# Rotation of the retention q and k: on GpSimd, or on VectorE in two steps

## The chip, the cores and the metric

The kernel runs on one core of one Trainium2 chip. The metric is device time in microseconds (us) of one execution; lower is better. TensorE (PE) multiplies, VectorE (DVE), ScalarE (ACT) and GpSimd (POOL) do the elementwise work, and SyncE (SP), ACT and POOL issue the transfers (DMA).

## The reference, cut to what matters

Two layers of a hybrid decoder block on 256 tokens of width 1024, all in float32. Each layer has a SwiGLU half step, one combined projection into three branches (retention, sliding-window attention, attention into 256 memory tokens), a gated sum of the branches, an output projection and a second SwiGLU half step. The change concerns one step of the retention branch, the rotation of its q and k (4 heads of 128 each) by position:

```
def rotary(x):
    ...
    x1, x2 = x[..., :half], x[..., half:]
    return jnp.concatenate([x1 * cos - x2 * sin, x1 * sin + x2 * cos], axis=-1)
...
    q = rotary(q.astype(f32))
    k = rotary(k.astype(f32)) * (dk ** -0.5)
...
    s = jnp.einsum('bnchd,bnshd->bnhcs', qc, kc) * intra_decay
```

## The kernel before, in words

**Weights.** All large products run in three passes of TensorE (lines 761 to 763): each float32 weight is split into a high and a low part. A weight block of 128x2048 (1 MB) is loaded by SP into a slot of `raw` (three slots, here also `raw_x`), ACT makes `w_hi` from it (line 1169, two pieces of 128x1024), and DVE makes `w_lo` as the difference (line 1563, two pieces). Each of those pieces on DVE counts up the semaphore `weights_made`, on which SP's next loads wait. `w_hi` and `w_lo` have three slots too, so ACT and DVE make the weights of an item up to three items before TensorE uses them.

**Quarter sums.** Pairs of projections (`rk` is the pair of retention q and k) are computed with seven products in place of eight, numbered 1 to 7. For some of them the weight is a sum of two blocks, made by DVE (line 1560) or by a transfer of POOL that adds into the slot (line 668).

**Order.** The order inside the mixing part is one list of names, `SCHEDULE`, that every engine walks through, each doing its own part of each name. An engine does its instructions strictly in that order. A name like `rk:4` is a product, `rv0.1` the second half of a projection, and a plain name is a step. After an item's own work ACT and DVE make the weights that the item's freed slot takes. Around the change the list reads, before:

```
... pv0 rk:7 e1 rv0.0 s2 rk:4 rg:5 rot pt1 rg:1 rqt pv1 rv0.1 e2 s3 rv1.0 e3 rg:3 pt2 rg:6 ...
```

Of these, `rot` is the rotation; `rqt` transposes the rotated q on TensorE (line 818) and waits for it (semaphore `rotated`); `rkt`, some items later, does the same for k. `s2` and `s3` are scores of the sliding window (line 969), `e1` to `e3` their exponentials on ACT, `pt1` the transposes of the probabilities (line 981), and `pv0`, `pv1` the products with the values (lines 993 and 995), which DVE scales into `stA` (lines 1816, 1818, 1825). The small products rotate through four PSUM banks, so that `s2` takes a bank that `pv0` leaves, and `s3` one that `pv1` leaves: TensorE can't start `s3` before DVE has done line 1825 of `pv1`.

**The rotation.** It is done in place in `stB`, per 128 tokens and for q and k (four tiles of 128x512 a layer): `rot_a` is the tile times the cosines (line 699), `rot_b` the swapped halves times the sines (line 702, two instructions of 4 heads x 64), and their sum goes back to `stB` (line 706). The scratch `rot_a` and `rot_b` lies over memory from which the memory values were written out by the transfer `mv_kept<-mv_made`, so the first tile waits for that (`mv_stored`).

Of the kernel before, what the change touches and what calls it, by code (L numbers as in the profile page):

```python
# [30 lines left out]
P = 128  # L31
# [42 lines left out]
MIX_PAIRS = {"sq": ("sq0", "sq1"), "rk": ("rq0", "rk0"), "rv": ("rv0", "rv1"), "rg": ("rg0", "rg1"),  # L74
             "gs": ("gs0", "gs1"), "mq": ("mq0", "mq1"), "gr": ("gr0", "gr1"), "gm": ("gm0", "gm1")}
SCHEDULE = """
mk0.1+xt0 mk1.0+xt1 mk1.1 skv.0 sq0.0 S_sum sq1.0 S_hi S_lo mkt sq1.1 sq0.1 skt mv0.0 sqt rk:5 mv0.1 s0 mv1.0 s1 e0 rk:1 rk:3 pt0 rk:6 mv1.1 mv_out rk:2 pv0 rk:7 e1 rv0.0 s2 rk:4 rg:5 rot pt1 rg:1 rqt pv1 rv0.1 e2 s3 rv1.0 e3 rg:3 pt2 rg:6 rv1.1 rkt rg:7 pv2 rg:2 rg:4 pt3 gs:5 rs gs:1 pv3 gs:3 gs:6 st gs:2 gs:7 us0.0 gs:4 ro us0.1 us1.0 mq1.0 us1.1 re mq1.1 mq0.0 mq0.1 gr:5 mqt gr:3 gr:1 rt mkT_in gr:6 gm0.0 gr:7 gr:2 gr:4 mv_in ms me ur0.0 mn x_in ur0.1 gm0.1 ur1.0 mpt gm1.0 ur1.1 mpv um0.0 um0.1 gm1.1 um1.0 mg0 um1.1 wo0.0 mg1 wo1.0 wo0.1 wo1.1+yt0
""".split()

PAIR_OF, STEPS = {}, []  # L80
# [278 lines left out]
def build(nc, x_in, mem_in, memt_in, stream, gains_in, gfin_in, rot_in, decay_in, mask_in, ident_in, out):  # L359
# [6 lines left out]
    with ctx:  # L366
# [279 lines left out]
        @block.gpsimd  # L646
        def _(pool):
            pool.memset(still[:, :], 0.0).then_inc(still_ready, 1)
            pool.memset(eps[:, :], EPS).then_inc(pool_step, 1)
            pool.memset(mhalf[:, :], -0.5).then_inc(pool_step, 1)  # L650
            pool.memset(minus[:, :], -1.0).then_inc(pool_step, 1)
            pool.wait_ge(pool_step, 3)

            def inv_rms(dst, src, n, done, step):

                pool.tensor_tensor(dst[:, 0:n], src[:, 0:n], eps[:, 0:n], ALU.add).then_inc(pool_step, 1)
                pool.wait_ge(pool_step, step)
# [12 lines left out]

            def quarters_after(l, i):
                if ITEMS[l][i] == ("down", 2, DOWNS[l, 2][-1]):
                    quarters_after(l, i - 1)
                for o in split_after[l * NI + i]:
                    add_quarters(o)

            PER = 5 + 4 * 3
            for l in range(DEPTH):
                def at(n):
                    return l * PER + (3 + n)  # L680

                def ffn(f):
                    for s in ffn_steps(l, f):
                        if s[0] != "gt" and s != ("down", f, DOWNS[l, f][-2]):
                            quarters_after(l, AT[l][s])

                n = 3

                def rotate(qk, t):
                    nonlocal n  # L690
                    pool.wait_ge(*done_of(l, ("rq0", "rk0")[qk], t))
                    src = stB[:, t, qk * BLK:(qk + 1) * BLK].rearrange("p (h d) -> p h d", h=RET_H)
                    av = rot_a[:, :].rearrange("p (h d) -> p h d", h=RET_H)
                    bv = rot_b[:, :].rearrange("p (h d) -> p h d", h=RET_H)
                    half = RET_DK // 2
                    cos = rot[:, 0, t].unsqueeze(1).broadcast_to([P, RET_H, P])
                    if n > 3:
                        pool.wait_ge(rotated, l * 4 + (qk * TT + t))
                    pool.tensor_tensor(av, src, cos, ALU.mult).then_inc(pool_step, 1)
                    for lo, hi in ((0, half), (half, 0)):  # L700
                        sin = rot[:, 1, t, lo:lo + half].unsqueeze(1).broadcast_to([P, RET_H, half])
                        pool.tensor_tensor(bv[:, :, lo:lo + half], src[:, :, hi:hi + half], sin, ALU.mult)\
                            .then_inc(pool_step, 1)
                    n += 3
                    pool.wait_ge(pool_step, at(n))
                    pool.tensor_tensor(src, av, bv, ALU.add).then_inc(rotated, 1)

                pool.wait_ge(msq_ready, l * 3 * TT + TT)
                inv_rms(rstd, msq, TT, rstd_ready, at(1))
                if l == 0:  # L710
                    for dst, src in ((rot, rot_in), (decay, decay_in), (mask, mask_in)):
                        pool.dma_start(dst[:], src).then_inc(tables_loaded, 16)
                ffn(1)
                pool.wait_ge(mem_msq_ready, l * TT + TT)
                inv_rms(rstd_mem, msq_mem, TT, rstd_mem_ready, at(2))
                pool.wait_ge(msq_ready, l * 3 * TT + 2 * TT)
                inv_rms(rstd, msq, TT, rstd_ready, at(3))
                pool.wait_ge(rstd_ready, l * 3 + 2)
                pool.tensor_tensor(minus_rstd[:, :], rstd[:, :], minus[:, :], ALU.mult).then_inc(minus_ready, 1)
                pool.wait_ge(tables_loaded, 16 * 3)  # L720
                for s in STEPS:
                    if s[0] != "step":
                        quarters_after(l, AT[l][s if s[0] == "prod" else ("mix", s[1])])
                    elif s[1] == "rot":
                        pool.wait_ge(mv_stored, 16 * (l + 1))
                        for qk in range(2):
                            for t in range(TT):
                                rotate(qk, t)
                    elif s[1] == "ro":
                        pool.wait_ge(retsq_ready, l * 2 * RET_H + 2 * RET_H)  # L730
                        inv_rms(rstd_r, msq_r, 2 * RET_H, retstd_ready, at(n + 1))
                pool.wait_ge(msq_ready, l * 3 * TT + 3 * TT)
                inv_rms(rstd, msq, TT, rstd_ready, at(n + 2))
                assert n + 2 == PER
                ffn(2)

            for t in range(TT):
                r = rstd[:, t:t + 1]
                pool.wait_ge(end_mean, t + 1)
                pool.tensor_tensor(r, r, mhalf[:, 0:1], ALU.pow).then_inc(end_rstd, 1)  # L740
# [795 lines left out]
        def _(dve):  # L1536
# [177 lines left out]
            for l in range(DEPTH):  # L1714
# [39 lines left out]
                def product(k, n):  # L1754

                    if n not in (2, 6, 7):
                        return
                    t, j = QUARTERS[n]
                    name, other = f"p0_{k}_{n}", {2: 1, 6: 3, 7: 5}[n]
                    buf = {"sq": stB, "rk": stB, "rv": rv, "rg": srg, "mq": stA}.get(k, gates)  # L1760
                    dst = buf[:, t, j * BLK:(j + 1) * BLK]
                    taken = snap_late[other][:, :] if k in ("gr", "gm") else dst
                    dve.wait_ge(minus_ready, l + 1)
                    dve.wait_ge(*full(l, name))
                    dve.wait_ge(*out_of(l, f"p0_{k}_{other}"))
                    if n == 2:
                        i = nc.vector.scalar_tensor_tensor(dst, bank(name)[:, :], rstd[:, t:t + 1], taken, op0=ALU.mult, op1=ALU.add)
                    else:
                        i = nc.vector.scalar_tensor_tensor(dst, bank(name)[:, :], minus_rstd[:, t:t + 1], taken, op0=ALU.mult, op1=ALU.subtract)
                    i.then_inc(free(name), 1)  # L1770

                def step(s):
                    if s == "S_sum":
                        left_sums(l, 0, hM)
                    elif s == "S_lo":
                        left_parts(l, 0)
# [205 lines left out]
```

## Time and profile before

| | |
|---|---|
| time, median of 3 runs | 1474.6 us (1473.6 to 1475.37) |
| time of the profiled execution | 1475.33 us |
| its span, from first to last instruction | 1473.5 us |
| busy: TensorE / VectorE / ScalarE / GpSimd | 98% / 77% / 65% / 8% of the span |
| mean granted TensorE clock | 0.992 of full speed |

The span is what the trace shows of the execution; 1.8 us of its time lie around it. TensorE works nearly without a gap, so what matters are the few places at which it waits, what it waits for there, and the stretches behind them in which its clock is lower. The layers are alike: the rotation comes at about 295 us in the first and at about 1020 us in the second.

### The profile page before, as it was taken

Reading aid. Unit: us, or ns where it says so; the run is one execution under the profiler, and the core shown is the slowest. Engines: PE = TensorE matmul, PEld = TensorE weight load, DVE = VectorE, ACT = ScalarE, POOL = GpSimd, SP = SyncE. Lnnn points to the kernel's source line nnn. Section 1 sums busy time; section 2 is a strip of 40 time slices with the busy share of each in tenths; the row PEclk is TensorE's granted clock in tenths of the full one; section 3 lists DMA queues with packets and bytes.
Section 4 is the critical chain, followed back from the end, with each engine's and each line's share of the span. In section 5 each row is a group of like instructions: output and inputs, shape, how many; then the busy total and the mean of one; then the engine's idle time right before and its main releaser. Section 6 shows DMA issues by size and latency. Waiting matters only on the chain.

```text
span 1473.5 us, 17927 instructions
## 1 busy us (share of the span) xinstructions
PE 1442.0 (98%) x6838; PEld 1195.7 (81%) x6838; DVE 1134.8 (77%) x1266; ACT 960.0 (65%) x1412; POOL 116.7 (8%) x125
## 2 busy tenths in 40 slices
PE   8999999989999999999999999999899999999997
PEld 6888888868888888888888888888688888888886
DVE  6998755797677658798789986568786885688994
ACT  6777666667647447676677775668675664476673
POOL 0000000070000000000000000002500000010000
PEclk9999999999999999999999999999999999999999
DMA  9999648855847557889939987567666564778881
GB/s 368 261 280 275 249 158 287 230 150 170 257 130 274 196 184 273 260 250 308 324 118 286 296 222 278 203 207 222 168 193 236 177 235 159 294 205 270 276 267 43
DMA packets 49380, 340.37 MB, mean 231 GB/s; under 512 B 5552, under 2 KB 6192, under 8 KB 8848
## 3 DMA queue, kind: packets, MB, share of 16 engines
q1 hardware_dynamic: 37392, 259.54, 46.8%
q0 software_dynamic: 8624, 61.74, 21.6%
q10 hardware_dynamic: 3280, 17.95, 3.2%
q8 instruction: 55, 0.90, 0.2%
q14 instruction: 29, 0.24, 0.0%
HBM read 331.87 MB, written 7.34 MB: 230 GB/s over the span
## 4 chain that ended last, share of the span: by engine, by line
PE 86%; DVE 7%; DMA 3%; ACT 2%; issue 1%; SPq 1%; POOLq 0%; POOL 0%; DVEq 0%; ACTq 0%
PE bank L761 26%; PE bank L763 26%; PE bank L762 26%; DVE w_lo L1563 4%; PE bank L818 4%; DMA raw<-in_stream 2%; DMA raw_q<-in_stream 1%; ACT w_hi L1169 1%; PE bank L1096 1%; PE bank L1078 1%; DVE raw_x L1560 1%; PE bank L969 1%; ACT prob L1469 1%; PE bank L995 0%; SPq L622 0%
## 5 line engine op out<-in xcount | busy, mean ns | idle before, releaser
L1563 DVE TENSOR_TENSOR w_lo<-raw,w_hi 128x1024 fp32r<-128x1024 f32 x356 | 428.0, 1245 | 179.4 <-ACT w_hi L1169 178.8
L1169 ACT ACTIVATE w_hi<-raw 128x1024 fp32r<-128x1024 f32 x356 | 356.8, 1053 | 210.7 <-PE bank L763 192.1
L761 PE MATMUL bank<-w_hi,hT_lo 128*128 128x512 f32 (+1 forms) x716 | 280.7, 392 | 0.5 <-DVE hT_lo L1587 0.2
L763 PE MATMUL bank<-w_lo,hT_hi 128*128 128x512 f32 (+1 forms) x716 | 276.3, 386 | 0.0
L762 PE MATMUL bank<-w_hi,hT_hi 128*128 128x512 f32 (+1 forms) x716 | 276.2, 386 | 0.0
L761 PEld LDWEIGHTS bank<-w_hi,hT_lo 128*128 128x128 f32 x716 | 135.1, 189 | 30.9 <-issue 3.7
L763 PEld LDWEIGHTS bank<-w_lo,hT_hi 128*128 128x128 f32 x716 | 134.9, 188 | 27.4
L762 PEld LDWEIGHTS bank<-w_hi,hT_hi 128*128 128x128 f32 x716 | 135.2, 189 | 25.4
L761 PE MATMUL bank<-w_hi,S_lo 128*128 128x512 f32 x340 | 135.4, 398 | 1.1 <-ACT snap L1250 0.8
L763 PE MATMUL bank<-w_lo,S_hi 128*128 128x512 f32 x340 | 132.8, 390 | 0.0
L762 PE MATMUL bank<-w_hi,S_hi 128*128 128x512 f32 x340 | 132.4, 389 | 0.0
L761 PE MATMUL bank<-w_hi,bT_lo 128*128 128x512 f32 x320 | 126.8, 396 | 0.0
L763 PE MATMUL bank<-w_lo,bT_hi 128*128 128x512 f32 x320 | 124.7, 390 | 0.0
L762 PE MATMUL bank<-w_hi,bT_hi 128*128 128x512 f32 x320 | 124.6, 389 | 0.0
L761 PE MATMUL bank<-w_hi,gT_lo 128*128 128x512 f32 x256 | 101.3, 396 | 4.6 <-DVE gT_lo L1581 4.5
L763 PE MATMUL bank<-w_lo,gT_hi 128*128 128x512 f32 x256 | 100.5, 392 | 0.0
L762 PE MATMUL bank<-w_hi,gT_hi 128*128 128x512 f32 x256 | 100.2, 391 | 0.0
L1563 DVE TENSOR_TENSOR w_lo<-raw_q,w_hi 128x1024 fp32r<-128x1024 f32 x70 | 82.5, 1220 | 13.0 <-ACT w_hi L1169 13.0
L1563 DVE TENSOR_TENSOR w_lo<-raw_b,w_hi 128x1024 fp32r<-128x1024 f32 x68 | 80.1, 1219 | 9.6 <-ACT w_hi L1169 9.6
L1169 ACT ACTIVATE w_hi<-raw_b 128x1024 fp32r<-128x1024 f32 x68 | 68.3, 1054 | 24.9 <-PE bank L763 11.8
L1169 ACT ACTIVATE w_hi<-raw_q 128x1024 fp32r<-128x1024 f32 x70 | 70.3, 1055 | 21.6 <-PE bank L763 16.6
L761 PEld LDWEIGHTS bank<-w_hi,S_lo 128*128 128x128 f32 x340 | 63.9, 188 | 14.3 <-ACT snap L1250 1.5
(229 smaller groups left out, 2461.4 us busy)
## 6 DMA issues: line engine op xcount, KB each, us to landing
raw<-in_stream SPq DMA_DIRECT2D x158, 1024.0 KB, 5.8
raw_b<-in_stream SPq DMA_DIRECT2D x33, 1024.0 KB, 8.0
raw_q<-in_stream SPq DMA_DIRECT2D x33, 1024.0 KB, 9.0
raw<-in_stream POOLq DMA_DIRECT2D x30, 1024.0 KB, 9.1
raw_x<-in_stream SPq DMA_DIRECT2D x20, 1024.0 KB, 5.1
raw_b<-in_stream POOLq DMA_DIRECT2D x15, 1024.0 KB, 10.2
raw_q<-in_stream POOLq DMA_DIRECT2D x11, 1024.0 KB, 12.0
raw<-in_stream SPq DMA_DIRECT2D x8, 256.0 KB, 6.9
```

The source lines that it names most:

```text
L761: nc.tensor.matmul(dst, xl, wh[:, a:b], start=first, stop=False, skip_group_check=more)
L762: nc.tensor.matmul(dst, xh, wh[:, a:b], start=False, stop=False, skip_group_check=more)
L763: return nc.tensor.matmul(dst, xh, wl[:, a:b], start=False, stop=last, skip_group_check=more)
L818: last = nc.tensor.transpose(bank(name)[:, at:at + P], src(t, k0 + j), ident[:, :])
L969: last = nc.tensor.matmul(bank(name)[:, i * n:(i + 1) * n], sqT[rows, head // 2, tokens(b)], skT[rows, head // (SWA_H // SWA_KV), 0:n], st ...
L1078: last = nc.tensor.matmul(bank(name)[:, t * MEM:(t + 1) * MEM], mqT[:, 2 * h + k, tokens(t)], mkT[:, 2 * h + k, :], start=k == 0, stop=k == 1)
L1096: last = nc.tensor.matmul(bank(name)[:, j * SEQ:(j + 1) * SEQ], mv[:, m, k * P:(k + 1) * P], mpT[:, h, m, :], start=m == 0, stop=m == 1)
L1169: nc.scalar.activation(slots(o)[0][:, part], raw_slot(s)[:, part], ACT.Copy).then_inc(hi_split, 1)
L1469: last = nc.scalar.activation(p, p, ACT.Exp, bias=snm[:, g % 2, i, b:b + 1], accum_out=ssum[:, g % 2, i, b:b + 1])
L1560: nc.vector.tensor_tensor(raw_slot(to[0]), raw_slot(to[0]), raw_slot(plus[0]), ALU.add).then_inc(weights_made, 1)
L1563: nc.vector.tensor_tensor(lo[:, part], raw_slot(s)[:, part], hi[:, part].bitcast(F32), ALU.subtract)\
```

## The change

The step `rot` of GpSimd becomes two steps, `rotq` and `rotk`, of VectorE, at the same place of the list. VectorE does the same four instructions a tile, with the same waits; within a tile the last one waits for the second multiplication by the sines through `dve_step`, and each tile's first waits for the sum of the tile before (`rotated`). Two waits are added in front of VectorE's products of the gates `gr` and `gm`; they wait for VectorE's own earlier work.

```diff
-... e1 rv0.0 s2 rk:4 rg:5 rot pt1 rg:1 rqt pv1 ...
+... e1 rv0.0 s2 rk:4 rg:5 rotq rotk pt1 rg:1 rqt pv1 ...
...
-                    elif s[1] == "rot":
-                        pool.wait_ge(mv_stored, 16 * (l + 1))
-                        for qk in range(2):
-                            for t in range(TT):
-                                rotate(qk, t)
...
+                    if k == "gr":
+                        dve.wait_ge(*out_of(l, f"us{j}t{t}"))
+                    if k == "gm":
+                        dve.wait_ge(gates_used, l * 8 + (TT * j + t + 1))
...
+                def rotate(qk, t):
+
+                    dve.wait_ge(*done_of(l, ("rq0", "rk0")[qk], t))
+                    src = stB[:, t, qk * BLK:(qk + 1) * BLK].rearrange("p (h d) -> p h d", h=RET_H)
+                    av = rot_a[:, :].rearrange("p (h d) -> p h d", h=RET_H)
+                    bv = rot_b[:, :].rearrange("p (h d) -> p h d", h=RET_H)
+                    half = RET_DK // 2
+                    if qk or t:
+                        dve.wait_ge(rotated, l * 4 + (qk * TT + t))
+                    nc.vector.tensor_tensor(av, src, rot[:, 0, t].unsqueeze(1).broadcast_to([P, RET_H, P]), ALU.mult)
+                    for lo, hi in ((0, half), (half, 0)):
+                        sin = rot[:, 1, t, lo:lo + half].unsqueeze(1).broadcast_to([P, RET_H, half])
+                        i = nc.vector.tensor_tensor(bv[:, :, lo:lo + half], src[:, :, hi:hi + half], sin, ALU.mult)
+                    own(i)
+                    settled()
+                    nc.vector.tensor_tensor(src, av, bv, ALU.add).then_inc(rotated, 1)
+
                 def step(s):
-                    if s == "S_sum":
+                    if s in ("rotq", "rotk"):
+                        dve.wait_ge(mv_stored, 16 * (l + 1))
+                        for t in range(TT):
+                            rotate(int(s == "rotk"), t)
+                    elif s == "S_sum":
```

On VectorE, from the weights made behind `rk:4` and `rg:5` to the scaling of `pv1`, the kernel before has these rows (the brackets name the semaphores waited for):

```order
L1563 TENSOR_TENSOR w_lo<-raw,w_hi 128x1024 [waits hi_split] x4
L1560 TENSOR_TENSOR raw_x<-raw_x,raw 128x2048 [waits weights_made,raw_loaded2,raw_loaded7]
L1563 TENSOR_TENSOR w_lo<-raw,w_hi 128x1024 [waits hi_split] x2
L1816 TENSOR_TENSOR ssum<-ssum,sexp 128x8 [waits swa_exp]
L1818 RECIPROCAL ssum<-ssum 128x8 [waits dve_step]
L1825 TENSOR_TENSOR stA<-bank,ssum 128x256 [waits psum_full4,dve_step]
```

The changed kernel has at the same place (first tile of q, first of k, and what follows; line numbers are 27 or 2 lower here for the same code):

```order
L1536 TENSOR_TENSOR w_lo<-raw,w_hi 128x1024 [waits hi_split] x4
L1758 TENSOR_TENSOR rot_a<-stB,rot 128x512 [waits psum_free3,mv_stored]
L1761 TENSOR_TENSOR rot_b<-stB,rot 128x4x64 x2
L1764 TENSOR_TENSOR stB<-rot_a,rot_b 128x512 [waits dve_step]
...
L1758 TENSOR_TENSOR rot_a<-stB,rot 128x512 [waits rotated,psum_free2,mv_stored]
...
L1533 TENSOR_TENSOR raw_x<-raw_x,raw 128x2048 [waits weights_made,raw_loaded2,raw_loaded7]
L1536 TENSOR_TENSOR w_lo<-raw,w_hi 128x1024 [waits hi_split] x2
L1814 TENSOR_TENSOR ssum<-ssum,sexp 128x8 [waits swa_exp]
L1816 RECIPROCAL ssum<-ssum 128x8 [waits dve_step]
L1823 TENSOR_TENSOR stA<-bank,ssum 128x256 [waits psum_full4,dve_step]
```

Sixteen instructions a layer now stand in VectorE's queue between the four `w_lo` pieces and everything behind them; the order of the rest is as it was. On GpSimd, from the reciprocal of the norm on, the kernel before has

```order
L719 TENSOR_TENSOR minus_rstd<-rstd,minus 128x2
L668 DMA raw<-in_stream 128x2048 x3
L699 TENSOR_TENSOR rot_a<-stB,rot 128x512
L702 TENSOR_TENSOR rot_b<-stB,rot 128x4x64 x2
L706 TENSOR_TENSOR stB<-rot_a,rot_b 128x512
```

and the changed kernel

```order
L698 TENSOR_TENSOR minus_rstd<-rstd,minus 128x2
L668 DMA raw<-in_stream 128x2048 x4
L668 DMA raw_x<-in_stream 128x2048
L668 DMA raw<-in_stream 128x2048 x2
L656 TENSOR_TENSOR rstd_r<-msq_r,eps 128x8
```

so that GpSimd's fourth adding transfer no longer stands behind the rotation. TensorE's, ScalarE's and SyncE's rows are the same in both.

## Rows read from the trace of the kernel before

**Rows 1.** The page's busy time of each engine.

```profile
PE 1442.0 (98%) x6838; PEld 1195.7 (81%) x6838; DVE 1134.8 (77%) x1266; ACT 960.0 (65%) x1412; POOL 116.7 (8%) x125
```

**Rows 2.** Waits of TensorE: us in total, times, longest.

```profile
PE bank L969 <- DVE stA L1825: 13.8, 3, 6.7
```

**Rows 3.** Timeline, TensorE, both layers: start, us, instructions, [idle before <-releaser].

```profile
298.93 1.58 PE L969 MATMUL bank<-skT,sqT 64*128 64x128 f32 x16 [0.69 <-DVE stA L1825]
310.11 1.04 PE L818 MATMUL bank<-ident,stB 128*128 128x128 f32 x8
...
325.62 2.93 PE L969 MATMUL bank<-skT,sqT 64*128 64x128 f32 x16 [6.34 <-DVE stA L1825]
...
1035.02 1.03 PE L818 MATMUL bank<-ident,stB 128*128 128x128 f32 x8
...
1050.95 2.93 PE L969 MATMUL bank<-skT,sqT 64*128 64x128 f32 x16 [6.73 <-DVE stA L1825]
```

**Rows 4.** Timeline, VectorE around the rotation, first layer, then one row of the second.

```profile
291.45 2.29 DVE L1560 TENSOR_TENSOR raw_x<-raw_x,raw 128x2048 f32<-128x2048 f32 x1 [2.08 <-DMA raw<-in_stream]
...
301.93 2.35 DVE L1563 TENSOR_TENSOR w_lo<-raw,w_hi 128x1024 fp32r<-128x1024 f32 x2
...
308.56 7.91 DVE L1563 TENSOR_TENSOR w_lo<-raw,w_hi 128x1024 fp32r<-128x1024 f32 x4
316.39 3.37 DVE L1560 TENSOR_TENSOR raw_x<-raw_x,raw 128x2048 f32<-128x2048 f32 x1
319.69 3.41 DVE L1563 TENSOR_TENSOR w_lo<-raw,w_hi 128x1024 fp32r<-128x1024 f32 x2
...
324.72 0.76 DVE L1825 TENSOR_TENSOR stA<-bank,ssum 128x256 f32<-128x256 f32 x2 [0.23 <-DVE ssum L1818]
...
1035.21 6.78 DVE L1563 TENSOR_TENSOR w_lo<-raw,w_hi 128x1024 fp32r<-128x1024 f32 x4
```

**Rows 5.** Timeline, GpSimd: the rotation's first instruction, and the one behind its last.

```profile
294.77 1.29 POOL L699 TENSOR_TENSOR rot_a<-stB,rot 128x512 f32<-128x512 f32 x1 [22.07 <-DMA mv_kept<-mv_made]
...
324.17 0.89 POOL L668 DMA_DIRECT2D raw<-in_stream  x1
```

**Rows 6.** Single lines of VectorE: duration min/median/max in ns, first and last start.

```profile
L1563 DVE TENSOR_TENSOR w_lo<-raw,w_hi x356: 1208/1219/2341, 17.6 to 1446.7; 128x1024 fp32r<-128x1024 f32 x178
L1816 DVE TENSOR_TENSOR ssum<-ssum,sexp x8: 159/431/1253, 297.1 to 1097.5; 128x8 f32<-128x8 f32 x8
L1825 DVE TENSOR_TENSOR stA<-bank,ssum x16: 414/420/425, 298.0 to 1098.3; 128x256 f32<-128x256 f32 x16
L1811 DVE TENSOR_TENSOR ssink<-gains,smax x8: 159/160/1277, 268.7 to 1057.4; 128x8 f32<-128x8 f32 x8
```

**Rows 7.** Timeline, VectorE where 128x512 operations follow each other from SBUF.

```profile
230.09 0.69 DVE L1598 TENSOR_TENSOR S_sum<-hM 128x512 f32<-128x512 f32 x1
230.81 0.69 DVE L1600 SCALAR_TENSOR_TENSOR S_sum<-S_sum,hM 128x512 f32<-128x512 f32 x1
231.42 0.69 DVE L1602 TENSOR_TENSOR S_sum<-hM 128x512 f32<-128x512 f32 x1
```

**Rows 8.** Busy time by stretch; the column before the DMA share is the granted clock.

```profile
324.00:324.50 0.50, 0.00 (x0) 0.00 (x0) 0.45 (x2) 0.50 (x4) 0.50 (x2) 0.89 0.00 0
331.00:331.50 0.50, 0.50 (x3) 0.36 (x3) 0.50 (x1) 0.00 (x0) 0.00 (x0) 0.78 1.39 197
1048.00:1048.50 0.50, 0.00 (x0) 0.00 (x0) 0.50 (x1) 0.50 (x3) 0.50 (x1) 0.52 0.00 0
1054.50:1055.00 0.50, 0.50 (x3) 0.40 (x2) 0.50 (x2) 0.00 (x0) 0.00 (x0) 0.65 0.86 180
```

**Rows 9.** Timeline, ScalarE: high parts of the weights.

```profile
299.31 1.99 ACT L1169 ACTIVATE w_hi<-raw 128x1024 fp32r<-128x1024 f32 x2
...
335.60 2.01 ACT L1169 ACTIVATE w_hi<-raw 128x1024 fp32r<-128x1024 f32 x2 [10.10 <-PE bank L763]
...
1024.78 1.99 ACT L1169 ACTIVATE w_hi<-raw 128x1024 fp32r<-128x1024 f32 x2
```

More of the change, by code:

```diff
@@ L76 @@
 SCHEDULE = """
-mk0.1+xt0 mk1.0+xt1 mk1.1 skv.0 sq0.0 S_sum sq1.0 S_hi S_lo mkt sq1.1 sq0.1 skt mv0.0 sqt rk:5 mv0.1 s0 mv1.0 s1 e0 rk:1 rk:3 pt0 rk:6 mv1.1 mv_out rk:2 pv0 rk:7 e1 rv0.0 s2 rk:4 rg:5 rot pt1 rg:1 rqt pv1 rv0.1 e2 s3 rv1.0 e3 rg:3 pt2 rg:6 rv1.1 rkt rg:7 pv2 rg:2 rg:4 pt3 gs:5 rs gs:1 pv3 gs:3 gs:6 st gs:2 gs:7 us0.0 gs:4 ro us0.1 us1.0 mq1.0 us1.1 re mq1.1 mq0.0 mq0.1 gr:5 mqt gr:3 gr:1 rt mkT_in gr:6 gm0.0 gr:7 gr:2 gr:4 mv_in ms me ur0.0 mn x_in ur0.1 gm0.1 ur1.0 mpt gm1.0 ur1.1 mpv um0.0 um0.1 gm1.1 um1.0 mg0 um1.1 wo0.0 mg1 wo1.0 wo0.1 wo1.1+yt0
+mk0.1+xt0 mk1.0+xt1 mk1.1 skv.0 sq0.0 S_sum sq1.0 S_hi S_lo mkt sq1.1 sq0.1 skt mv0.0 sqt rk:5 mv0.1 s0 mv1.0 s1 e0 rk:1 rk:3 pt0 rk:6 mv1.1 mv_out rk:2 pv0 rk:7 e1 rv0.0 s2 rk:4 rg:5 rotq rotk pt1 rg:1 rqt pv1 rv0.1 e2 s3 rv1.0 e3 rg:3 pt2 rg:6 rv1.1 rkt rg:7 pv2 rg:2 rg:4 pt3 gs:5 rs gs:1 pv3 gs:3 gs:6 st gs:2 gs:7 us0.0 gs:4 ro us0.1 us1.0 mq1.0 us1.1 re mq1.1 mq0.0 mq0.1 gr:5 mqt gr:3 gr:1 rt mkT_in gr:6 gm0.0 gr:7 gr:2 gr:4 mv_in ms me ur0.0 mn x_in ur0.1 gm0.1 ur1.0 mpt gm1.0 ur1.1 mpv um0.0 um0.1 gm1.1 um1.0 mg0 um1.1 wo0.0 mg1 wo1.0 wo0.1 wo1.1+yt0
 """.split()
@@ L269 @@
 NG = G_SINK + SWA_H
-DVE_STEPS = 24
+DVE_STEPS = 28
 X_PARTS = [slice(0, BLK // 2), slice(BLK // 2, BLK), slice(BLK, D)]
@@ L675, in quarters_after @@
                     add_quarters(o)
-            PER = 5 + 4 * 3
+            PER = 5
             for l in range(DEPTH):
@@ L685, in ffn @@
                             quarters_after(l, AT[l][s])
[L687 to L706, printed above, removed]
                 pool.wait_ge(msq_ready, l * 3 * TT + TT)
@@ L723, in _ @@
                         quarters_after(l, AT[l][s if s[0] == "prod" else ("mix", s[1])])
-                    elif s[1] == "rot":
-                        pool.wait_ge(mv_stored, 16 * (l + 1))
-                        for qk in range(2):
-                            for t in range(TT):
-                                rotate(qk, t)
                     elif s[1] == "ro":
                         pool.wait_ge(retsq_ready, l * 2 * RET_H + 2 * RET_H)
-                        inv_rms(rstd_r, msq_r, 2 * RET_H, retstd_ready, at(n + 1))
+                        inv_rms(rstd_r, msq_r, 2 * RET_H, retstd_ready, at(4))
                 pool.wait_ge(msq_ready, l * 3 * TT + 3 * TT)
-                inv_rms(rstd, msq, TT, rstd_ready, at(n + 2))
-                assert n + 2 == PER
+                inv_rms(rstd, msq, TT, rstd_ready, at(PER))
                 ffn(2)
```

## The prediction

> **What bounds the kernel now.** I begin with the page's busy times: TensorE has 98% of the span [rows 1], so a change elsewhere counts only where it moves one of TensorE's waits. The view of waits shows what they are. Three waits of the scores (`s2`, `s3`) for VectorE's scaling `stA` come to 13.8 us [rows 2]. The timeline places them: 0.69 us at 298.93 and 6.34 us at 325.62 in the first layer, 6.73 us at 1050.95 in the second [rows 3]. All three fall beside or right behind the rotation, which GpSimd begins at 294.77 and leaves shortly before 324.17 [rows 5].
>
> Next comes VectorE's timeline at that place. From 301.93 on it has no idle time worth naming, but its instructions are longer than elsewhere. Four pieces of `w_lo` take 7.91 us, the sum `raw_x` 3.37 and two more pieces 3.41 [rows 4]. A piece takes 1.219 us in the median, a pair that nothing disturbs 2.35, and the same sum 2.29 when GpSimd is idle [rows 4, 6]; back to back, a piece costs 1.14 (it overlaps the next by 0.08) and the sum 2.21. So the three groups would take 4.64, 2.29 and 2.36 us, and the rotation beside them costs VectorE 3.27 + 1.08 + 1.05 = 5.4 us. Even tiny operations between two SBUF tiles suffer: `ssum` has a median of 0.43 and a maximum of 1.25 us against 0.16, `ssink` a maximum of 1.28 against 0.16 [rows 6]. VectorE's queue up to `stA` is what TensorE waits for, and GpSimd stretches it.
>
> The clock belongs to the wait. In the first layer it falls from full to half (2.4 to 1.2 GHz) at about 324.4, 5.1 us after TensorE stopped, and returns at about 331.2; in the second it falls at 1048.0 and returns at 1054.85 [rows 8]. Work runs at half speed from 325.62 to 331.2 and from 1050.95 to 1054.85, which loses half of these, 2.8 and 1.95 us. The place costs now 0.69 + 6.34 + 2.8 = 9.8 us in the first layer and 6.73 + 1.95 = 8.7 in the second.
>
> **The change, part by part.**
>
> *Price of the rotation on VectorE.* The trace before has no multiplication by a broadcast table here, so I take the nearest rows. A 128x512 operation takes 0.69 us; one that waits for its predecessor's result starts 0.72 behind it (0.03 of latency), one that doesn't 0.61 [rows 7]. A 128x256 operation with a broadcast operand takes 0.42, and a pair 0.76, so the first of a pair costs 0.34 [rows 4, 6]. A tile is cosines 0.61, first sines 0.34, second sines 0.42 + 0.03, sum 0.69 + 0.03: 2.12 us. q has two tiles, 4.2 us; q and k 8.4 us. Bounds: with no overlap at all 2.28 a tile (0.69 + 0.42 + 0.42 + 0.69 and 0.06), which makes q 0.3 us longer; with full overlap of every instruction 1.9 (twice 0.61 and 0.34), 0.4 shorter for q. I take 2.12, since each part is a row of the same kind and size.
>
> A rule of the Trainium skill ("VectorE: DVE Perf Modes", section on the TRN2 errata) would price an SBUF operation of N elements at 58 + N cycles of 0.96 GHz, hence 0.594 and 0.327 us, and a tile at 1.84. By it q would be 0.55 us shorter and the whole change 1.1 us better than my sum. The rows here show 0.69 for such an operation, and they decide.
>
> *VectorE's start in the first layer.* Without GpSimd's rotation the stretch from 294.77 on is shorter, but the pair at 301.93 can't start before ScalarE has the first half of its `w_hi`, made from 299.31 on in 1.05 us [rows 4, 9]; that is 300.4. So VectorE reaches the four pieces 1.5 us earlier, plus 0.1 for small operations stretched in between: 307.0 instead of 308.56 [rows 4]. Four pieces take 4.56 and the rotation starts at 311.5. The transfer that it waits for was done at 294.77 [rows 5], so that wait is free. q is ready at 315.7, and `rqt` can start 0.14 later, at 315.9 (the gap between the end of `stA` at 325.48 and the start at 325.62) [rows 3, 4].
>
> *The new wait.* TensorE reached `rqt` at 310.11 without waiting [rows 3]; now it comes 0.7 earlier, since the wait at 298.93 goes (its `stA` stands behind a stretched `ssum` [rows 6] and stretched pieces, which together give back more than 0.7). With its last product ending 0.16 after the next could start, TensorE stands from 309.6 to 315.9, 6.3 us. Queued behind are `pv1`, `rv0.1` and `s3`, 9.0 us of work (from 310.11 to 325.62 - 6.34 = 319.28, where the wait before `s3` began, less the 0.16) [rows 3]. Its clock will fall as it did for an idle time of the same length; I put down 2.5 us, between the two losses seen.
>
> *The old wait.* `rotk` 4.2, `raw_x` 2.21, two pieces 2.28, then `ssum`, the reciprocal and `stA` 1.2: `stA` is done at 315.7 + 9.9 = 325.6, as before (325.48). But TensorE comes to `s3` only at 315.9 + 9.0 + 2.5 = 327.4, so the 6.34 us there are gone. The price of `rotk` is covered by TensorE's own work, with 1.7 us to spare; without that cover each us of it would be a us of wait.
>
> *The second layer.* Four pieces started at 1035.21 [rows 4]. `ssum` and `ssink` were stretched by 1.1 us each [rows 6], and one pair of pieces between them too, but the pair behind that waits for ScalarE's half at 1024.78 + 1.05 [rows 9]; that makes 1.65 + 1.1 = 2.75 us earlier, 1032.5. Add 4.56 and 4.2: q at 1041.2, `rqt` at 1041.4 instead of 1035.02 [rows 3]. TensorE stands 6.2 us; `stA` is ready at 1051.1 and `s3` comes at 1041.4 + 9.0 + 2.5 = 1052.9, again without a wait.
>
> *The rest costs nothing.* GpSimd's fourth adding transfer may leave before 324.17 [rows 5]; nobody waited for it, ScalarE waiting for TensorE at 335.60 [rows 9]. ScalarE's `w_hi` of `raw_x` and `e2` move behind the later end of `rv0.1`, into its idle time of 10.1 us before 335.60 [rows 9]; if that were not there, they would delay the next weights by some 5 us. The added waits for `gr` and `gm` are for VectorE's own finished work. SP's next load waits for pieces that come 0.5 us later relative to TensorE, well ahead of need.
>
> **The sum.** First layer: 6.3 + 2.5 = 8.8 against 9.8, that is -1.0. Second: 6.2 + 2.5 = 8.7 against 8.7, 0. The profiled execution took 1475.33 us (span 1473.5 and 1.8 around it), which gives 1474.3; the median of the runs is 0.7 lower, so I say 1473.6 against 1474.6. The long wait is moved from `s3` to `rqt`, hardly shortened.
>
> **The rivals.**
> - *The clock stays up.* In the first layer it fell 5.1 us after TensorE stopped, in the second 3.8 [rows 3, 8]; had the fall come over 6.3 us after, the new wait would end before it. For that speaks only that the delay varies. Then `s3` waits for `stA` at 325.75, and the layer costs 325.75 less the 318.5 at which TensorE could have come, 7.2 us: -2.6 in the first and -1.5 in the second. In both layers 1470.5, in one about 1472.5.
> - *The stretching isn't GpSimd's doing* (slower). If the long `w_lo` and `raw_x` came from something else, such as transfers, the rotation would simply be put into the queue: q at 316.4 + 4.2, a wait of 10.5 us and 2.8 of clock, then `stA` at 325.5 + 8.4 = 333.9, 1.5 behind TensorE. That is +5 us in the first and +6 in the second, 1486. Against it: the stretched rows lie just where GpSimd computes, and the pair at 301.93, in its pause, took the usual 2.35 [rows 4, 5]. It decides from 1.5 us more a layer before q is ready.
> - *The queue behind is late* (slower). The `s3` masks on VectorE now end near 336.1, 0.5 after it would take up the weights of 335.60 [rows 9]. If loads behind these pieces landed late, each layer would lose 1 to 2 us: 1477.
> - *It does nothing at all.* If both waits keep their sum to within the 0.2% (2.9 us) that a measurement of this kernel can tell from no change, this can't be told from my forecast.
>
> **How the numbers follow.** Wait moved, sum kept: 0.63, with its own range of 1472.0 to 1475.5 (0.3 to 0.4 us a layer of q's price, 1 of the clock, 0.5 of the run). Clock stays up in a layer or both: 0.17, half of it beyond 0.2%. Stretching not relieved, in part or all: 0.10. Queue behind late: 0.10, half of it beyond. Over 0.2% faster also if the relief reaches work that I count as bound by ScalarE, 0.1 out of the first case. That makes faster 0.19, same 0.66, slower 0.15. The range goes down to the clock's case, 1470.4, and up to the late queue's, 1477.2.
>
> **What the profile after would show.** A wait of TensorE's line 818 for VectorE's `stB` of about 6 us at 309.5 and at 1035, and none over 1 us of line 969 for `stA`; `w_lo` with a maximum below 1.3 us everywhere; tiles of 2.1 us on VectorE; half clock for 4 to 6 us behind each wait. I am wrong if `s3` still waits for over 1 us behind a slow clock, if pieces stay stretched, or if a wait that stands in no row here appears behind 330.

## The result, and the profile after

The changed kernel takes 1479.89 us (median of 5 runs, 1477.81 to 1481.96) where the kernel before takes 1475.13 (5 runs, 1473.6 to 1475.42): a ratio of 1.0035, 95% interval 1.002 to 1.0049. It is slower, by 4.8 us. I had said 1473.6, in a range up to 1477.2.

The page's busy times and TensorE's view of waits (us in total, times, longest):
```profile
PE 1447.0 (98%) x6838; PEld 1200.4 (81%) x6838; DVE 1134.1 (77%) x1298; ACT 959.4 (65%) x1412; POOL 66.6 (5%) x93
```
```profile
PE bank L791 <- DVE stB L1764: 12.1, 2, 6.1
PE bank L734 <- DVE gT_lo L1554: 3.6, 1, 3.6
```
TensorE does the same 6838 instructions as in [rows 1], but they take 5.0 us more. The 13.8 us of waits for `stA` [rows 2] are gone; two waits for the rotated q in `stB` stand in their place. The timeline of TensorE, first layer and then the second, with the first product behind each wait and the first large one:
```profile
297.43 1.58 PE L942 MATMUL bank<-skT,sqT 64*128 64x128 f32 x16
...
314.81 1.97 PE L791 MATMUL bank<-ident,stB 128*128 128x128 f32 x8 [6.05 <-DVE stB L1764]
316.57 0.53 PE L966 MATMUL bank<-sv,pT 128*128 128x64 f32 x2
...
321.56 0.77 PE L734 MATMUL bank<-w_hi,hT_lo 128*128 128x512 f32 x1
...
324.22 0.40 PE L734 MATMUL bank<-w_hi,hT_lo 128*128 128x512 f32 x1
...
328.43 1.58 PE L942 MATMUL bank<-skT,sqT 64*128 64x128 f32 x16
...
1041.21 1.97 PE L791 MATMUL bank<-ident,stB 128*128 128x128 f32 x8 [6.00 <-DVE stB L1764]
```
Line 942 is `s2` and `s3` (line 969 in [rows 3]): neither waits now. Line 791 is `rqt`; its eight transposes took 1.04 us in [rows 3] and take 1.97 here. A large product takes 0.77 us at 321.56 and 0.40 at 324.22. That is the clock. Busy time by stretch, granted clock in the column before the DMA share:
```profile
313.00:314.00 1.00, 0.00 (x0) 0.00 (x0) 1.00 (x3) 0.00 (x0) 0.00 (x0) 0.96 1.16 467
...
318.00:323.00 5.00, 5.00 (x22) 4.71 (x22) 4.97 (x6) 0.00 (x0) 0.00 (x0) 0.50 0.00 0
324.00:324.50 0.50, 0.50 (x4) 0.39 (x3) 0.50 (x2) 0.00 (x0) 0.31 (x1) 0.84 0.00 0
1037.00:1038.00 1.00, 0.00 (x0) 0.00 (x0) 1.00 (x3) 0.82 (x1) 0.00 (x0) 0.77 0.99 418
...
1051.00:1051.50 0.50, 0.50 (x3) 0.37 (x2) 0.14 (x1) 0.00 (x0) 0.43 (x1) 0.80 0.00 0
```
A mean of 0.96 over one us means that the clock fell at 313.92, and 0.84 over half a us that it rose at 324.16; in the second layer it fell at 1037.54 and rose at 1051.2. Work ran at 1.2 GHz from 314.81 to 324.16 and from 1041.21 to 1051.2, 9.35 and 10.0 us, of which half is lost: 4.7 and 5.0. In the kernel before it was 2.8 and 1.95 [rows 8].

VectorE's timeline shows the relief and the new step:
```profile
305.94 4.63 DVE L1536 TENSOR_TENSOR w_lo<-raw,w_hi 128x1024 fp32r<-128x1024 f32 x4
310.48 0.69 DVE L1758 TENSOR_TENSOR rot_a<-stB,rot 128x512 f32<-128x512 f32 x1
311.09 0.76 DVE L1761 TENSOR_TENSOR rot_b<-stB,rot 128x256 f32<-128x256 f32 x2
311.88 0.69 DVE L1764 TENSOR_TENSOR stB<-rot_a,rot_b 128x512 f32<-128x512 f32 x1
312.67 0.69 DVE L1758 TENSOR_TENSOR rot_a<-stB,rot 128x512 f32<-128x512 f32 x1
...
314.07 0.69 DVE L1764 TENSOR_TENSOR stB<-rot_a,rot_b 128x512 f32<-128x512 f32 x1
...
319.09 2.28 DVE L1533 TENSOR_TENSOR raw_x<-raw_x,raw 128x2048 f32<-128x2048 f32 x1
321.29 2.35 DVE L1536 TENSOR_TENSOR w_lo<-raw,w_hi 128x1024 fp32r<-128x1024 f32 x2
...
323.99 0.76 DVE L1823 TENSOR_TENSOR stA<-bank,ssum 128x256 f32<-128x256 f32 x2
```
The three groups of [rows 4] went from 7.91, 3.37 and 3.41 us to 4.63, 2.28 and 2.35. `stA` is done at 324.75, before TensorE comes to `s3` at 328.43. VectorE did its part; the time went into TensorE's clock.

The place, from the waits and the half clock, costs 6.05 + 4.7 = 10.75 and 6.00 + 5.0 = 11.0, in all 21.75 us; before it was 9.8 + 8.7 = 18.5. That is +3.25. One wait elsewhere, for `gT_lo`, has 3.6 us here and had 4.5 before; in a second profile of the changed kernel (`e5_after_again`) it has 4.6, so it varies by itself. +3.25 - 0.9 gives +2.35; the two profiled executions differ by 2.5 (1477.81 against 1475.33). The second profile took 1478.93 us, +3.6: there the two waits are 6.15 and 6.14 and the work at half clock 9.3 and 10.1 us, so the place costs 22.0, +3.5. The medians differ by 4.8 and, in the 8 runs of `e5_after_again`, by 4.3; about 1 us of that has no row in either profile and stays open.

### The profile page after: what moved, and what is told of

Same layout as the page of the kernel before. It is cut to its first block, busy times and chain, and to the rows that moved or that the text cites. A ratio compares the mean times of both kernels' runs of the same rounds, so it can differ in the third digit from the quotient of the medians.

```text
span 1476.0 us, 17933 instructions
## 1 busy us (share of the span) xinstructions
PE 1447.0 (98%) x6838; PEld 1200.4 (81%) x6838; DVE 1134.1 (77%) x1298; ACT 959.4 (65%) x1412; POOL 66.6 (5%) x93
## 4 chain that ended last, share of the span: by engine, by line
PE 90%; DVE 4%; ACT 3%; DMA 2%; issue 1%; SPq 1%; POOLq 0%; POOL 0%; DVEq 0%; ACTq 0%
PE bank L734 27%; PE bank L736 27%; PE bank L735 27%; PE bank L791 4%; DVE w_lo L1536 1%; ACT w_hi L1142 1%; DMA raw_q<-in_stream 1%; PE bank L968 1%; PE bank L1051 1%; PE bank L1069 1%; DMA raw<-in_stream 1%; ACT prob L1442 1%; PE bank L966 0%; PE bank L942 0%; PE bank L954 0%
## 5 line engine op out<-in xcount | busy, mean ns | idle before, releaser
L1536 DVE TENSOR_TENSOR w_lo<-raw,w_hi 128x1024 fp32r<-128x1024 f32 x356 | 419.3, 1220 | 171.2 <-ACT w_hi L1142 170.4
L1142 ACT ACTIVATE w_hi<-raw_b 128x1024 fp32r<-128x1024 f32 x68 | 68.3, 1055 | 24.8 <-PE bank L736 11.8
L1142 ACT ACTIVATE w_hi<-raw_q 128x1024 fp32r<-128x1024 f32 x70 | 70.2, 1055 | 19.9 <-PE bank L736 15.8
L1536 DVE TENSOR_TENSOR w_lo<-raw_x,w_hi 128x1024 fp32r<-128x1024 f32 x48 | 56.6, 1220 | 32.0 <-ACT w_hi L1142 31.7
```

Source lines behind the costliest of these rows:

```text
L1142: nc.scalar.activation(slots(o)[0][:, part], raw_slot(s)[:, part], ACT.Copy).then_inc(hi_split, 1)
L1536: nc.vector.tensor_tensor(lo[:, part], raw_slot(s)[:, part], hi[:, part].bitcast(F32), ALU.subtract)\
```

## The experiments

Theory: the wait was moved as forecast, and the loss is that the clock stays low for longer behind it, because `rqt` and `pv1` follow, small products (8 transposes of 128 columns, then 24 records of 64 columns), where `s3` (16 records of 128) and then large products followed before. Counts here are those of the trace, in which each small float32 product of `pv1`, `s3` and e10 stands as two records. Rivals: the rotation on VectorE costs in other ways (its length, a queue behind), or the longer stretch belongs to the length of the wait. All ratios are against the kernel before on the same chip, whose median there was 1475.46 (e1 to e4), 1475.0 (e5 to e8), 1475.16 (e9 to e11) and 1475.61 us (e12).

| run | median us (runs) | ratio | interval |
|---|---|---|---|
| e1_after_warm | 1472.11 (7) | 0.9981 | 0.9968 to 0.9994 |
| e2_before_warm | 1471.17 (6) | 0.9966 | 0.9953 to 0.9979 |
| e3_no_rotation | 1468.72 (5) | 0.9943 | 0.9923 to 0.9963 |
| e4_dense_first | 1483.32 (4) | 1.0053 | 1.0039 to 1.0067 |
| e5_after_again | 1479.31 (8) | 1.0023 | 1.0011 to 1.0034 |
| e6_q_same_k_late | 1467.07 (5) | 0.9943 | 0.9931 to 0.9956 |
| e7_stA_first | 1472.46 (11) | 0.9982 | 0.9973 to 0.9991 |
| e8_all_behind_s3 | 1466.16 (5) | 0.994 | 0.9927 to 0.9952 |
| e9_order_alone | 1475.52 (11) | 0.9997 | 0.9988 to 1.0006 |
| e10_small_behind_wait | 1503.26 (2) | 1.019 | 1.0172 to 1.0207 |
| e11_all_hidden | 1464.46 (6) | 0.9927 | 0.9914 to 0.9939 |
| e12_rqt_later | 1461.06 (4) | 0.9903 | 0.9887 to 0.992 |

### What is the clock worth: e1 and e2

24 products without use fill the wait, ahead of `rqt` in the changed kernel:
```diff
+                        if s == "rqt":
+                            pe.wait_ge(*room(l, "rqt_0"))
+                            for _ in range(24):
+                                nc.tensor.matmul(bank("rqt_0")[:, :], still[:, 0:P], still[:, :], start=True, stop=True)
```


> The changed kernel, with 24 idle matmuls of 128x512 (bf16 zeros, into a bank that the transposes then overwrite) that TensorE runs just before it waits for the rotated q. Nothing else changes and the output is the same. Theory C (the clock): the change kept the idle time (12.1 us in two waits, against 13.8 before) but the stretch of half clock behind each wait grew to 9.3 and 10.2 us of work, a loss of 4.7 + 5.1 us against 2.8 + 1.95. With TensorE busy in the wait its clock stays at full speed, and the time falls by about 9.8 us or more, to 1468 to 1470 us, with a spread as small as before. Rival Q (something in the queues behind the rotation is late, the clock is only a by-product): the time stays at 1478 to 1480 us.

The same lines with bank `s3_1`, ahead of the wait of `s3`, in the kernel before:

> The kernel before, with the same 24 idle matmuls just before TensorE waits for the banks of s3. Theory C: this gives back the 2.8 + 1.95 us of the clock, so 1475.1 - 4.8 = about 1470.4 us; the changed kernel with warm matmuls is then 1 to 2 us faster than this one, which is the saving that the prediction forecast with a clock loss that it took as equal. Rival Q: both fillings do the same, so the changed kernel stays some 4 us slower than this one.

The timeline of TensorE of e1:
```profile
309.31 5.35 PE L1014 MATMUL bank<-still 128*128 128x512 bf16 x24
315.52 1.09 PE L791 MATMUL bank<-ident,stB 128*128 128x128 f32 x8 [0.86 <-DVE stB L1768]
...
325.60 1.58 PE L942 MATMUL bank<-skT,sqT 64*128 64x128 f32 x16 [0.83 <-DVE stA L1827]
```
The filler starts when TensorE comes and ends before q is ready, so it hides nothing of the wait; the clock stays at full speed through both places (1.00 from 300 to 325 and from 1030 to 1055). The changed kernel goes from 4.3 to 4.8 us above the kernel before to 3.35 below it (1472.11 against 1475.46), a gain of some 8 us; the one before gains 4.3 (1475.46 to 1471.17). By rows it should be 9.7, less the 1.7 of a new wait of `s3` for `stA`, which is 8.0, and 4.75. With the clock equal the kernels stand 0.9 us apart where 4.3 to 4.8 had stood: most of the loss is clock. I had expected e1 some us lower and below e2; but `s3` waits for `stA` in both (it starts at 325.60 in e1 and at 325.29 in e2), so the moved wait gains nothing.

### What the rotation costs in all: e3

```diff
-                    nc.vector.tensor_tensor(av, src, rot[:, 0, t].unsqueeze(1).broadcast_to([P, RET_H, P]), ALU.mult)
...
-                    nc.vector.tensor_tensor(src, av, bv, ALU.add).then_inc(rotated, 1)
+                    nc.vector.tensor_scalar(src[:, 0:1, 0:1], src[:, 0:1, 0:1], 1.0, None, ALU.mult).then_inc(rotated, 1)
```


> The changed kernel without the rotation: each tile's four instructions are one that touches a single column (the output is that of unrotated q and k). It gives the price of the whole place. Theory C and the prediction's model: VectorE's queue up to stA is 8.4 us shorter and not stretched by GpSimd, stA is done about 316.5, before TensorE comes to s3 (about 317.7), so no wait of TensorE is left at either place and no clock is lost: 1475.1 - 9.8 - 8.7 = about 1456.6 us. If another queue (transfers, ScalarE) were next behind VectorE, waits of TensorE for it would show, and the time would be 1460 us or more.

The median is 12 us above the forecast, the profiled execution (1462.81) 6.2 us. A wait that I had not seen is left, for the instruction that now stands for the rotation:
```profile
PE bank L791 <- DVE stB L1758: 4.5, 2, 2.3
```
So the wait of 6.0 us isn't the rotation of q alone. In the changed kernel TensorE stopped at 308.76 and VectorE began the rotation at 310.48: 1.7 us are the four pieces of `w_lo` ahead of it in the queue, and 4.3 the rotation. (The 2.2 us of e3 are those pieces and the short instructions that stand for the rotation.) These waits are 4.5 of the 6.2 us. Three of the other executions took 1468.72 us or more, with a mean granted clock of 0.990 to 0.995 against 0.997 in the profiled one; why stays open.

### Does the work behind the wait set the clock: e4, e5, e10

e4 puts large products behind `rqt`:
```diff
-... rg:1 rqt pv1 rv0.1 e2 s3 ...
+... rg:1 rqt rv0.1 pv1 e2 s3 ...
```


> The changed kernel with pv1 and rv0.1 exchanged in the list (rqt rv0.1 pv1), so that after the wait of 6 us and the 8 transposes TensorE runs 24 matmuls of 512 columns at once, and the 24 small ones of pv1 (64 columns each) after them. Theory C, in the form that the small work behind the wait is what keeps the clock down: half clock lasts about 7 us from its fall, as in the kernel before (6.8 in both layers), not 10.2. Rival C2 (the length of the stretch is chance, or hangs on the idle time alone): it lasts 10.2 us again or varies without regard to the work. The time itself says little, since s3 now waits about 3 us for a later stA: 1478 to 1482 us.

e5 is the changed kernel once more.

> The changed kernel once more, on the same chip as the reorderings, with a profile of its own. Theory C: TensorE waits again about 6 us at rqt in each layer and nowhere else at this place, and a stretch of half clock of 10 us or more begins in or behind each wait; the time is 1478 to 1482 us. If the longer stretches of half clock (10.24 and 13.65 us in the first profile against 6.83 in the kernel before) were chance, this profile shows one or both at 6.83 us.

e4's timeline of TensorE, and then its busy time by stretch (the clock before the DMA share):
```profile
316.00 1.97 PE L791 MATMUL bank<-ident,stB 128*128 128x128 f32 x8 [6.22 <-DVE stB L1764]
...
330.23 2.06 PE L942 MATMUL bank<-skT,sqT 64*128 64x128 f32 x16 [2.69 <-DVE stA L1823]
```
```profile
314.00:314.50 0.50, 0.00 (x0) 0.00 (x0) 0.50 (x2) 0.00 (x0) 0.00 (x0) 0.62 0.77 328
316.00:320.00 4.00, 4.00 (x14) 3.52 (x15) 3.75 (x8) 1.19 (x2) 0.00 (x0) 0.50 0.08 27
320.50:321.00 0.50, 0.50 (x3) 0.40 (x2) 0.50 (x1) 0.00 (x0) 0.00 (x0) 0.55 0.00 0
```
The wait is as long as in the changed kernel. The clock fell at 314.12 and rose at 320.95, 6.8 us, and in the second layer it was 6.8 us too (1044.57 to 1051.40). In e5 it fell at 315.08 and 1038.70 and rose at 325.32 and 1052.36:
```profile
315.00:315.50 0.50, 0.00 (x0) 0.00 (x0) 0.47 (x2) 0.00 (x0) 0.00 (x0) 0.58 0.82 328
325.00:325.50 0.50, 0.50 (x3) 0.40 (x2) 0.47 (x2) 0.00 (x0) 0.10 (x1) 0.68 0.00 0
1038.50:1039.00 0.50, 0.00 (x0) 0.00 (x0) 0.50 (x3) 0.22 (x1) 0.00 (x0) 0.70 1.16 492
1052.00:1052.50 0.50, 0.50 (x3) 0.36 (x3) 0.17 (x1) 0.00 (x0) 0.47 (x1) 0.64 0.00 0
```
That repeats the 10.2 and 13.65 us of the first profile exactly. The wait was the same and the order behind it other, and the stretch was 3.4 to 6.8 us shorter, so its length is not a matter of the wait alone. A stretch can begin inside the wait, and what costs is only the work in it, from the end of the wait on: 4.95 and 5.7 us in e4, 9.3 and 10.1 in e5, 5.6 and 3.9 in the kernel before. The 8 transposes stand behind the wait in e4 as well, so what differs is the place of `pv1`'s 64-column products. The kernel as a whole is slower still, more than I had expected: TensorE now waits a second time, 2.7 us a layer for `stA`, and a second half-clock stretch of 3.4 us follows.

e10 asks the same of the kernel before, with small products in place of large ones behind the wait of `s3`:
```diff
+                    if g == 3:
+                        for i in range(32):
+                            nc.tensor.matmul(bank("s3_1")[:, 0:HD], sqT[:, i % 8, 0:P], sqT[:, 0, 0:HD], start=True, stop=True)
```


> The kernel before, with 32 added matmuls of 64 columns (idle ones, into a bank that s3 then overwrites) between TensorE's wait before s3 and the scores. Only the work that follows the wait is changed, the idle time (6.3 and 6.7 us) is not. Theory C: the stretch of half clock, 6.83 us in both layers in the kernel before, grows to 10.2 us or more in both. Rival C2 (chance, or the idle time alone): it stays at 6.83. The time grows by what the added matmuls take, some 4 to 7 us a layer, besides the clock, so it tells nothing.

Its timeline and busy time by stretch:
```profile
325.10 13.89 PE L965 MATMUL bank<-sqT 128*128 128x64 f32 x64 [7.00 <-DVE stA L1828]
338.92 2.83 PE L972 MATMUL bank<-skT,sqT 64*128 64x128 f32 x16
341.68 0.50 PE L761 MATMUL bank<-w_hi,hT_lo 128*128 128x512 f32 x1
```
```profile
325.00:339.00 14.00, 13.90 (x66) 13.81 (x66) 2.22 (x2) 0.00 (x0) 0.88 (x1) 0.50 0.78 150
341.00:341.50 0.50, 0.50 (x4) 0.13 (x2) 0.00 (x0) 0.00 (x0) 0.00 (x0) 0.50 0.00 0
341.50:342.00 0.50, 0.50 (x3) 0.30 (x2) 0.21 (x1) 0.00 (x0) 0.00 (x0) 0.97 0.00 0
```
TensorE reads as busy all through, and yet its clock stays at half for the 14 us of small products and nearly all of `s3` behind them, 20.5 us in each layer against 6.8. The waits are 7.0 and 6.7 us, near the 6.34 and 6.73 of [rows 3]. With e4 this shows the theory from both sides. It also narrows it: in the first layer the clock is back at 341.52, in the scores of `s3` (128 columns) and ahead of the first large product at 341.68; in the second layer it came back at 1082.22, 2 us into the large ones. So it is the 64-column products that went with the low clock in these runs; that only large products bring it back isn't shown.

### Where else the steps can stand: e9, then e6, e7, e8, e11 and e12

Each line is the part of the list that changes; e9 keeps the rotation on GpSimd.
```
after  rg:5 rotq rotk pt1 rg:1 rqt pv1 rv0.1 e2 s3 rv1.0 e3 rg:3 pt2 rg:6 rv1.1 rkt
e9     rg:5 rot pt1 rg:1 pv1 rv0.1 rqt e2 s3 rv1.0 e3 rg:3 pt2 rg:6 rv1.1 rkt
e6     rg:5 rotq pt1 rg:1 pv1 rv0.1 rqt e2 s3 rotk rv1.0 e3 rg:3 pt2 rg:6 rv1.1 rkt
e7     rg:5 pt1 rg:1 pv1 rotq rv0.1 e2 s3 rv1.0 rqt e3 rg:3 pt2 rg:6 rotk rv1.1 rkt
e8     rg:5 pt1 rg:1 pv1 rv0.1 e2 s3 rotq rv1.0 e3 rg:3 rqt pt2 rotk rg:6 rv1.1 rkt
e11    rg:5 pt1 rg:1 pv1 rotq rv0.1 e2 s3 rotk rv1.0 rqt e3 rg:3 pt2 rg:6 rv1.1 rkt
e12    rg:5 pt1 rg:1 pv1 rv0.1 e2 s3 rotq rv1.0 e3 rg:3 pt2 rotk rg:6 rqt rv1.1 rkt
```


> The kernel before, with the rotation left on GpSimd, and only rqt moved behind rv0.1 (list ... rg:5 rot pt1 rg:1 pv1 rv0.1 rqt e2 s3 ...). It tells whether the gain of e6 comes from the order alone. Theory W: no. VectorE's queue up to stA is as long and as stretched as before (stA at about 325.5), TensorE never waited at rqt in this kernel, and s3 waits for stA some 6 us as before: 1475 us, within 0.2%. Rival: moving rqt alone gives e6's 1467.

e9 gives nothing: `s3` waits for `stA` 6.03 and 5.55 us, as it did. While GpSimd rotates, TensorE waits for the same stretched queue of VectorE, at both places of `rqt` that were tried.

> The changed kernel with the list ... rg:5 rotq pt1 rg:1 pv1 rv0.1 rqt e2 s3 rotk rv1.0 ...: the rotation of q stays where it is on VectorE, TensorE does pv1 and rv0.1 (8.1 us) before rqt, and the rotation of k goes behind s3. Theory W (what costs is that q's rotation stands before VectorE's work for pv1 while nothing of TensorE's stands before rqt): the wait at rqt vanishes, s3 waits 2.8 us for stA (rotq 4.2, the sum 2.2, two pieces 2.3, the scaling 1.2 behind 310.5), the clock stays up, and s3 starts at about 320.5 instead of 328.4: 8 us a layer, so 1464 us. Rival: if the k rotation behind s3 delays the weights of rv1.1, a new wait of 2 to 4 us a layer shows on line 734 and the time is 1468 to 1472.

> The list is ... rg:5 pt1 rg:1 pv1 rotq rv0.1 e2 s3 rv1.0 rqt e3 rg:3 pt2 rg:6 rotk rv1.1 rkt ...: VectorE scales pv1 first (stA at about 316.2) and then rotates q, TensorE comes to rqt a whole projection later, and k is rotated behind rg:6. Theory W: no wait of TensorE at s3 or rqt at all, s3 starts at about 317, 11.5 us earlier a layer than in the changed kernel: 1456 to 1458 us, no half clock in the middle of the kernel. Rival: VectorE has no idle time left between 301 and 333 us, so the weights of rv1.1 or a transfer behind them become the next wait: 1460 to 1466.

> As the one before, with the rotation of q behind the masks of s3 (list ... rg:1 pv1 rv0.1 e2 s3 rotq rv1.0 e3 rg:3 rqt pt2 rotk rg:6 rv1.1 rkt ...). Theory W: s3 as early as there, but rqt comes at about 326.5 while VectorE has q only at 329.2 (masks until 325.0, then 4.2), a wait of 2 to 3 us a layer: 1460 to 1463 us, slower than e7 by about 4.

All three beat the kernel before, and each shows one wait more. The views of waits of e6, e7 and e8, in this order:
```profile
PE bank L942 <- ACT rqT L1369: 5.7, 2, 2.9
```
```profile
PE bank L791 <- DVE stB L1764: 10.1, 2, 5.0
```
```profile
PE bank L791 <- DVE stB L1764: 5.4, 2, 2.7
```
In e6 `s3` waits for ScalarE's copy of the transposed q, which ends 0.7 us behind `stA`; the median is 3 us above the forecast. In e7 TensorE comes to `rkt` before VectorE has rotated k, which stands behind `rg:6`'s pieces; I had looked only at the place of `s3`, and missed by 15 us. In e8 q comes 2.7 us late for `rqt`, and the clock is low for 3.4 us behind each of these waits; the median is 3 us above the upper end of the forecast, and below e7, not above it.

> The changed kernel with the list ... rg:5 pt1 rg:1 pv1 rotq rv0.1 e2 s3 rotk rv1.0 rqt e3 rg:3 pt2 rg:6 rv1.1 rkt ...: q as in e7 (behind VectorE's scaling of pv1), k as in e6 (behind the masks of s3), rqt where q is long ready. Theory W: no wait of TensorE at s3, rqt or rkt over 0.5 us, so e8's time less its two waits of 2.7 us and the clock lost behind them (two stretches of 3.41 us at half clock, 1.7 each): 1457.5 us, or 1457 to 1460. Rival: the weights of rv1.1 or the transfers behind them are the next to be late, as VectorE has no idle time from 301 to 333 us: 1461 or more, with a wait of line 734.

e11 has no wait left for `stA` or `stB`, but two of 1.0 us for the decayed scores `sdec`, made by VectorE, which some 20 us before waits 3.1 and 3.7 us for a load and has no idle time in between. Behind the second of them, in `pv3`, the clock falls for 3.4 us; behind the first it doesn't. The rest of the 7 us between forecast and median is open.

> e8 with rqt two items later (list ... rg:1 pv1 rv0.1 e2 s3 rotq rv1.0 e3 rg:3 pt2 rotk rg:6 rqt rv1.1 rkt ...), so that TensorE comes to it after q is ready. e8 still waited 2.7 us a layer at rqt and had a stretch of 3.41 us at half clock behind each; e11, which hid all three waits, got only 1464.5 because VectorE's masks of rs came 1 us late in both layers (wait for sdec) behind a sum that waited 3.7 us for its transfer. Theory W: 1466.2 - 5.4 - 3.4 = 1457 to 1458 us if nothing else is near. Rival T (transfers and VectorE's queue behind the place are now the next limit, as in e11): 1461 to 1465 us with a wait for sdec, or for weights on line 734.

e12's timeline of TensorE and two stretches of its clock:
```profile
317.51 1.58 PE L942 MATMUL bank<-skT,sqT 64*128 64x128 f32 x16
...
333.46 0.66 PE L791 MATMUL bank<-ident,stB 128*128 128x128 f32 x4 [1.46 <-ACT pT L1369]
...
339.42 1.03 PE L791 MATMUL bank<-ident,stB 128*128 128x128 f32 x8
```
```profile
305.00:360.00 55.00, 53.27 (x297) 44.94 (x296) 51.26 (x68) 43.21 (x82) 2.59 (x3) 1.00 0.62 182
1025.00:1080.00 55.00, 53.26 (x299) 44.92 (x297) 50.93 (x70) 42.39 (x83) 3.41 (x4) 1.00 0.63 180
```
`s3` starts at 317.51 without a wait, since `stA` is ready at 316.5 with no rotation ahead of it, and the clock never falls at the place. What is left is 1.5 us a layer in `rqt` for ScalarE, a wait that neither case of the expectation named; the median is 3 us above the forecast. The place costs some 3.5 us in all (two waits of 1.5, two of 0.3) where it cost 18.5; the 15.0 between them answer to the 14.55 of the medians. At 1461.06 us this is the best version: 1.0% below the kernel before, 1.2 to 1.3% below the changed one.

## Why the prediction was wrong

- *The relief was right.* Groups of 4.64, 2.29 and 2.36 us were forecast, and 4.63, 2.28 and 2.35 came. `w_lo` from `raw` has a maximum of 1.227 us (2.341 in [rows 6]), `ssum` 0.161 (1.253). The rival that the stretching isn't GpSimd's doing is out.
- *The price of the tile was nearly right:* 2.19 us from start to start (310.48 to 312.67) against 2.12; the first instruction of the next tile starts 0.10 behind the end of the sum, not 0.03. The rule of the Trainium skill ("VectorE: DVE Perf Modes", section on the TRN2 errata) gave an estimate of 1.84, further off.
- *VectorE's start* was a us earlier than forecast in the first layer (310.48 against 311.5), and 0.2 earlier in the second (1036.88 against 1037.06), where q came as forecast: `rqt` at 1041.21 against 1041.4. In the first layer most of that was there ahead of the place: VectorE's sum `raw_x` at 291.45 in [rows 4] started at 290.46. TensorE came earlier there too, so *the new wait* is 6.05 and 6.00 against 6.3 and 6.2.
- *The old wait is gone* in both layers, as forecast, with more to spare than I gave it: `stA` was ready 3.7 us ahead of `s3` (324.75 and 328.43, for forecasts of 325.6 and 327.4).
- *The step that failed* is this one: "Its clock will fall as it did for an idle time of the same length; I put down 2.5 us, between the two losses seen." The fall came much as before, 5.2 and 2.3 us after TensorE stopped. The way back came later: the loss measured 4.7 and 5.0 us, and the half clock behind the waits, for which I had said 4 to 6 us, 9.35 and 10.0. In the kernel before, large products follow the 16 records of `s3` behind the wait [rows 3, 8]; here 8 transposes and 24 records of 64 columns come first, and e4 and e10 show the clock low for longer where such products stand. I took the length of the wait for what sets the loss, and didn't look at what stands behind it. With 4.7 and 5.0 in place of twice 2.5 my sum of 1473.6 becomes 1478.3, 1.6 below the median.
- *The rivals.* In "the clock stays up" the place was right and the sign wrong; e1 made it happen and gave 1472.1, where the rival said 1470.5. (Its "in one about 1472.5" is a slip: -2.6 and 0, or -1.0 and -1.5, from 1474.6 make 1472.0 or 1472.1.) "The queue behind is late" didn't come: the next weights at 335.77 (335.60 in [rows 9]) find ScalarE idle for a us, and no new wait stands behind 330. No case of mine held a loss of clock above the two seen; a bound for that price would have needed a row at which small work follows a wait, and none stood there.

## What to carry to other kernels

A wait of TensorE costs its idle time and, where the clock falls, half of the work until it is back on top, and that second part depends on the work queued behind the wait: have large products there, and not a run of 64-column ones. When a step is moved to another in-order engine, first ask what on that queue should stand ahead of it: here the same 8.6 us of VectorE's time a layer made the kernel slower ahead of the result that TensorE needed first, and faster behind it. Then look at all its consumers, since e7's late k undid most of what its early `stA` had gained.

## What was unexpected of the hardware

- After a wait of 6.0 to 7.0 us the half-clock stretch was 6.8 us with large products early behind it (before, e4), 10.2 and 13.65 with 8 transposes and 24 records of 64 columns first (after, the same in two profiles), 20.5 with 64 records of 64 columns first (e10). That TensorE's busy share was full from the end of the wait on told nothing of its clock.
- Short waits differ. In e11 one of 1.0 us, followed by small products, had the clock fall two us into them, and its twin in the other layer did not; of e6's two waits of 2.9 us one did; those of 2.7 in e4 and e8 all did, those of 1.5 in e12 did not.
- 24 products of 512 columns in bf16, 5.35 us of work without use, kept the clock up through such a wait, and were worth 4.3 us in the kernel before and some 8 in the changed one.
- GpSimd's two-input operations lengthen VectorE's where both inputs lie in SBUF; the four masks of `prob<-bank,mask`, with one input in PSUM, took 1.94 us beside GpSimd's rotation (at 304.20, before) as without it (at 301.66, after). With the rotation gone from the place, 14.69 us of three groups became 9.26, and an operation on 128x8 elements went from at most 1.25 us to 0.16.
